# Twelve conditioning groups of a two-layer diffusion backbone: ten of them placed anew between attention, linear attention and three norms

## The reference

```python
def ada_mod(cond, w, b):
    mod = jax.nn.silu(cond) @ w + b
    return [m[:, None, :] for m in jnp.split(mod, 6, axis=-1)]
...
    for l in range(DEPTH):
        sc1, scl1, gc1, sc2, scl2, gc2 = ada_mod(cond_ctx, ada_w[l], ada_b[l])
        sl1, sll1, gl1, sl2, sll2, gl2 = ada_mod(c, ada_w[l], ada_b[l])
        hc = modulate(rmsnorm(xc, norm_mix[l]), sc1, scl1)
        hl = modulate(rmsnorm(xl, norm_mix[l]), sl1, sll1)
...
        xc = xc + gc1 * oc
        xl = xl + gl1 * ol
        xc = xc + gc2 * hier_moe(modulate(rmsnorm(xc, norm_ffn[l]), sc2, scl2), *moe)
        xl = xl + gl2 * hier_moe(modulate(rmsnorm(xl, norm_ffn[l]), sl2, sll2), *moe)
```

## Time and profile before

| | |
|---|---|
| times of the three runs | 1988.06, 2001.43, 2002.7 us; median 2001.43 |
| time of the profiled execution | 2004.93 us |
| its span in the trace | 2003.1 us, mean granted PE clock 0.892 |
| PE busy | 1653.6 us (83%), x14360 |
| DVE, ACT, POOL busy | 601.6 (30%), 466.1 (23%), 229.0 us (11%) |
| queue of the weight stream | 288.89 MB, 37.9% of the 16 engines' span |
| products of the 12 groups (L315) | 60.5 us, x768, idle before them 59.3 us |

### The profile page before, as it was taken

One profiled execution on the slowest core, in us unless ns is written; L12 is line 12 of the kernel. 1 busy time (PEld: TensorE's weight loads), 2 busy tenths in 40 slices (PEclk: granted clock), 3 DMA queues, 4 the chain that ended last, 5 costly groups with the idle time before them and its releaser, 6 DMA issues. The chain is left out here.

```text
span 2003.1 us, 35164 instructions
## 1 busy us (share of the span) xinstructions
PE 1653.6 (83%) x14360; PEld 1221.1 (61%) x14361; DVE 601.6 (30%) x1419; ACT 466.1 (23%) x1058; POOL 229.0 (11%) x218
## 2 busy tenths in 40 slices
PE   2996956849999999639995888888875799999991
PEld 1553544436788788415544777777753577877871
DVE  2005654140111111260023566766623201111114
ACT  2114511022000010020033556555412110100002
POOL 0000110000000000100007255555300000000001
PEclk8997987959999999759996789989987799999995
DMA  8323664400788888702300000000022048888862
GB/s 324 125 96 118 257 254 174 168 11 19 314 322 318 315 315 310 287 22 105 105 0 3 4 5 5 5 5 5 5 107 74 0 176 327 305 315 329 311 240 103
DMA packets 49921, 314.77 MB, mean 157 GB/s; under 512 B 6192, under 2 KB 9584, under 8 KB 14480
## 3 DMA queue, kind: packets, MB, share of 16 engines
q1 hardware_dynamic: 43200, 288.89, 37.9%
q10 hardware_dynamic: 4880, 17.96, 2.2%
q0 software_dynamic: 1728, 6.29, 0.9%
HBM read 298.05 MB, written 15.07 MB: 156 GB/s over the span
## 5 line engine op out<-in xcount | busy, mean ns | idle before, releaser
L1260 PEld LDWEIGHTS ps<-arena,ring 128*128 128x128 f32 x4096 | 468.3, 194 | 21.7 <-issue 21.7
L1260 PE MATMUL ps<-arena,ring 128*128 x4096 | 468.0, 277 | 5.3 <-issue 5.3
L1272 PE MATMUL ps<-ring,arena 128*96 128x512 f32 x512 | 225.0, 592 | 0.0
L292 PE MATMUL ps<-HT,ring 128*128 128x384 f32 x544 | 179.7, 494 | 15.5 <-PEq L358 8.2
L1332 DVE TENSOR_TENSOR arena<-arena,ps 128x96 f32<-128x96 f32 x128 | 32.6, 254 | 496.8 <-ACT arena L1299 496.8
L292 PEld LDWEIGHTS ps<-HT,ring 128*128 128x128 f32 x544 | 104.8, 193 | 90.0 <-issue 20.2
L1272 PEld LDWEIGHTS ps<-ring,arena 128*96 128x96 f32 x512 | 81.0, 163 | 119.2 <-issue 119.2
L292 PE MATMUL ps<-arena,ring 128*128 128x384 f32 x384 | 125.9, 492 | 23.7 <-DVEq L1525 23.7
L1299 ACT ACTIVATE arena<-ps 128x96 f32<-128x96 f32 x128 | 32.2, 251 | 476.7 <-PE ps L1260 476.5
L1359 POOL DMA_INDIRECT arena<-moe_rows,arena x12 | 11.6, 969 | 1059.0 <-DMA moe_rows<-arena 1056.0
L292 PEld LDWEIGHTS ps<-arena,ring 128*128 128x128 f32 x384 | 73.8, 193 | 76.3 <-DVEq L1525 24.8
(11 more groups left out here) (308 smaller groups left out, 1980.0 us busy)
## 6 DMA issues: line engine op xcount, KB each, us to landing
ring<-wstream SPq DMA_DIRECT2D x272, 1024.0 KB, 6.7
moe_rows<-arena ACTq DMA_DIRECT2D x32, 384.0 KB, 6.8
consts<-cst ACTq DMA_DIRECT2D x1, 1648.5 KB, 17.1
XT<-xT ACTq DMA_DIRECT2D x1, 1536.0 KB, 11.1
yT<-HT ACTq DMA_DIRECT2D x1, 1536.0 KB, 5.1
arena<-wa SPq DMA_DIRECT2D x1, 1024.0 KB, 4.8
arena<-rcst SPq DMA_DIRECT2D x2, 448.0 KB, 3.8
ring<-zrwkv SPq DMA_DIRECT2D x16, 32.0 KB, 2.0
```

What stands on the lines that cost most here:

```text
L292: mm = pe.matmul(bank(m % 8), w[:, k, m % 2 * P:m % 2 * P + P], rhs[:, k, :], start=k == 0, stop=k == KC - 1)
L1260: mm = pe.matmul(bank(f % 2, CAP, CAP * w), wt[:, k, f % 2 * P:f % 2 * P + P], TOK[:, k, bass.ds(first, CAP)], start=k == 0, stop=k == KC - 1)
L1272: mm = pe.matmul(bank(4 + j, 512)[0:CAP], HIDG[:, f, :], wt[:, f, :], start=f == 0, stop=f == 3)
```

## The change

Group by group: attention takes five groups (2 to 6) and in every fifth step from step 1 on, where it had four in every sixth from step 2 on; linear attention takes two (7 and 8) where it had three; the tail none where it had three; the norm before MoE 0 takes group 9; the first norm of layer 1 takes groups 10 and 11. The tiles are laid out in the new order: groups 2 to 8, the output projection, group 9, MoE 0, groups 10 and 11, RWKV. In a norm, the products of the first group stand before PE's sum, its `ada_act` after the squares, its turn behind the sum and its `ada_dve` between L463 and the wait for the root. The second group of a norm has its products and turn behind that on PE, its `ada_act` after the modulation of chunk 3 on ACT and its `ada_dve` at the end of DVE's order.

```diff
--- before.py
+++ after.py
@@ -53,15 +53,18 @@
 QUAD = 4
 N_QUADS = N_ADA // QUAD
 QUADS_NOW = 2
+QUADS_MIXER, QUADS_RKV = 7, 2
 N_IN = 10
 N_OUT = 4
 N_MOE = NE * 6
 AT_ADA = 0
 AT_IN = AT_ADA + QUAD * QUADS_NOW
 AT_ADA_LATE = AT_IN + N_IN
-AT_OUT = AT_ADA_LATE + N_ADA - QUAD * QUADS_NOW
-AT_MOE0 = AT_OUT + N_OUT
-AT_RKV = AT_MOE0 + N_MOE
+AT_OUT = AT_ADA_LATE + QUAD * QUADS_MIXER
+AT_ADA_LAST = AT_OUT + N_OUT
+AT_MOE0 = AT_ADA_LAST + N_ADA - QUAD * (QUADS_NOW + QUADS_MIXER + QUADS_RKV)
+AT_ADA_RKV = AT_MOE0 + N_MOE
+AT_RKV = AT_ADA_RKV + QUAD * QUADS_RKV
 AT_LORA = AT_RKV + 12
 AT_GATE = AT_LORA + 1
 AT_WO = AT_GATE + 1
@@ -414,7 +417,7 @@
                 ada_dve(dve, 1, 4)
                 dve.sem_inc(s_rs, 1)
 
-        def norm_block(l, w, end, save=None):
+        def norm_block(l, w, end, quads=()):
 
             n = norms[0]
             norms[0] += 1
@@ -428,6 +431,8 @@
                 def _(act):
                     for k in range(KC):
                         act.activation(HT[:, k, :], XT[:, k, :], ACT.Square).then_inc(s_sq, 1)
+                    for q in quads[:1]:
+                        ada_act(act, q, 2 + q % 2)
                     act.wait_ge(s_var, n + 1)
                     act.activation(VAR, VAR, ACT.Sqrt).then_inc(s_sd, 1)
                     for k in range(KC):
@@ -440,6 +445,11 @@
                             act_o.inc(act.activation(HT[:, k, a:b], HT[:, k, a:b], ACT.Identity,
                                                      bias=mod[:, l, 3 * w, k, c:c + 1],
                                                      scale=gain[:, l, w, k, c:c + 1]))
+                        if k == 3:
+                            for q in quads[1:2]:
+                                ada_act(act, q, 2 + q % 2)
+                    for q in quads[2:]:
+                        ada_act(act, q, 2 + q % 2)
                     act_o.wait()
                     if l is None:
                         act.dma_start(yT, HT_[:, :]).then_inc(out_sem, 16)
@@ -448,9 +458,15 @@
 
                 @block.tensor
                 def _(pe):
-
+                    for q in quads[:1]:
+                        ada_pe_products(pe, q, 2 + q % 2)
                     pe.wait_ge(s_sqs, n + 1)
                     pe.matmul(bank(0), ones, RS, start=True, stop=True).then_inc(s_ss, 1)
+                    for q in quads[:1]:
+                        ada_pe_turn(pe, q, 4 + q % 2)
+                    for q in quads[1:]:
+                        ada_pe_products(pe, q, 2 + q % 2)
+                        ada_pe_turn(pe, q, 4 + q % 2)
 
                 @block.vector
                 def _(dve):
@@ -461,10 +477,14 @@
                     dve.sem_inc(s_sqs, 1)
                     dve.wait_ge(s_ss, n + 1)
                     dve.tensor_scalar(VAR, bank(0), 1.0 / D, EPS, ALU.mult, ALU.add).then_inc(s_var, 1)
+                    for q in quads[:1]:
+                        ada_dve(dve, q, 4 + q % 2)
                     dve.wait_ge(s_sd, n + 1)
                     dve_o(dve.reciprocal(RS, VAR))
                     for k in range(KC):
                         dve.tensor_tensor(HT[:, k, :], XT[:, k, :], RS, ALU.mult).then_inc(s_xn, 1)
+                    for q in quads[1:]:
+                        ada_dve(dve, q, 4 + q % 2)
 
 
 
@@ -645,10 +665,10 @@
             def keys(b):
                 return CTX if b < 0 else T
 
-            first_quad, quads_here = QUADS_NOW, 4
+            first_quad, quads_here = QUADS_NOW, 5
 
             def quad_at(step, u):
-                q, at = divmod(u - 2 - step, 6)
+                q, at = divmod(u - 1 - step, 5)
                 return first_quad + q if at == 0 and 0 <= q < quads_here else None
 
             @block.sync
@@ -814,7 +834,7 @@
             def flat(v):
                 return v.rearrange("p r d t -> p (r d t)")
 
-            gla_quads = (6, 7, 8)
+            gla_quads = (7, 8)
 
             @block.sync
             def _(sp):
@@ -979,7 +999,6 @@
                                             sem("gla_variance_ready"), sem("gla_std_ready"))
         O4 = area(at_aq, 4 * T)
         SQ4 = area(at_aq + 4 * T, 4 * T)
-        tail_quads = (9, 10, 11)
         with nc.Block() as block:
             @block.sync
             def _(sp):
@@ -994,25 +1013,19 @@
                 dve.tensor_scalar(SQ4.rearrange("p (h t) -> p h t", h=4),
                                   ps[:, 0:2048].rearrange("p (h t) -> p h t", h=4)[:, :, 0:T],
                                   1.0 / GV, EPS, ALU.mult, ALU.add).then_inc(s_gv, 1)
-                ada_dve(dve, tail_quads[0], 4 + tail_quads[0] % 2)
                 dve.wait_ge(s_gsd, 1)
                 dve_o(dve.reciprocal(SQ4, SQ4))
                 dve_o(dve.scalar_tensor_tensor(out=SQ4, in0=SQ4, scalar=V[:, V_GNORM:V_GNORM + 1], in1=O4,
                                                op0=ALU.mult, op1=ALU.mult))
                 dve_o(dve.tensor_tensor(OT[:, 0:4].rearrange("p h t -> p (h t)"), SQ4, SG.rearrange("p h t -> p (h t)"),
                                         ALU.mult))
-                for q in tail_quads[1:]:
-                    ada_dve(dve, q, 4 + q % 2)
 
             @block.scalar
             def _(act):
                 act.wait_ge(s_go2, 1)
                 act.activation(SQ4, O4, ACT.Square).then_inc(s_gsq, 1)
-                ada_act(act, tail_quads[0], 6 + tail_quads[0] % 2)
                 act.wait_ge(s_gv, 1)
                 act.activation(SQ4, SQ4, ACT.Sqrt).then_inc(s_gsd, 1)
-                for q in tail_quads[1:]:
-                    ada_act(act, q, 6 + q % 2)
 
             @block.gpsimd
             def _(pool):
@@ -1020,15 +1033,10 @@
 
             @block.tensor
             def _(pe):
-                ada_pe_products(pe, tail_quads[0], 6 + tail_quads[0] % 2)
                 pe.wait_ge(s_gsq, 1)
                 for h in range(4):
                     mm = pe.matmul(bank(h), ones, SQ4[:, T * h:T * h + T], start=True, stop=True)
                 mm.then_inc(s_gss, 1)
-                ada_pe_turn(pe, tail_quads[0], 4 + tail_quads[0] % 2)
-                for q in tail_quads[1:]:
-                    ada_pe_products(pe, q, 6 + q % 2)
-                    ada_pe_turn(pe, q, 4 + q % 2)
 
 
         def out_block(l, at, src, end, name):
@@ -1470,11 +1478,11 @@
 
             return router_sems + expert_sems
 
-        norm_block(0, 1, AT_MOE0 + RING)
-        moe0_sems = moe_block(0, AT_MOE0, AT_RKV + RING)
-
-
-        norm_block(1, 0, AT_RKV + RING)
+        norm_block(0, 1, AT_MOE0 + RING, quads=(9,))
+        moe0_sems = moe_block(0, AT_MOE0, AT_ADA_RKV + RING)
+
+
+        norm_block(1, 0, AT_RKV + RING, quads=(10, 11))
         a_[0] = 0
         XX = area(take(KC * T), KC * T, k=KC, t=T)
         XM = [area(take(KC * T), KC * T, k=KC, t=T) for _ in range(2)]
@@ -2181,7 +2189,13 @@
 
 def ada_tile(q, j):
 
-    return AT_ADA + QUAD * q + j if q < QUADS_NOW else AT_ADA_LATE + QUAD * (q - QUADS_NOW) + j
+    if q < QUADS_NOW:
+        return AT_ADA + QUAD * q + j
+    if q < QUADS_NOW + QUADS_MIXER:
+        return AT_ADA_LATE + QUAD * (q - QUADS_NOW) + j
+    if q < N_QUADS - QUADS_RKV:
+        return AT_ADA_LAST + QUAD * (q - QUADS_NOW - QUADS_MIXER) + j
+    return AT_ADA_RKV + QUAD * (q - N_QUADS + QUADS_RKV) + j
 
 
 def cols(v):
@@ -2237,7 +2251,7 @@
     w_in = np.zeros((D, 2560), np.float32)
     w_in[:, :IN_W] = f["ev_w_in"][0]
     w[AT_IN:AT_ADA_LATE] = tiles_of(w_in)
-    w[AT_OUT:AT_MOE0] = tiles_of(f["ev_w_out"][0])
+    w[AT_OUT:AT_ADA_LAST] = tiles_of(f["ev_w_out"][0])
     for l, at in ((0, AT_MOE0), (1, AT_MOE1)):
         for e in range(NE):
             t = at + 6 * e

```

## The result

| | before | after |
|---|---|---|
| median of 20 runs | 1993.63 us | 2004.62 us |
| lowest and highest | 1984.88, 2003.15 | 1998.22, 2008.5 |
| ratio, 95% interval | | 1.0047 [1.0029, 1.0064], that is +9.4 us (+5.8 to +12.8) |
| span of the profiled execution | 2003.1 us | 2005.2 us |
| PE busy, granted clock | 1653.6 us, 0.892 | 1664.9 us, 0.889 |

What follows compares the result with a forecast made beforehand. Each block is bounded by the engine that ends last, with the weight stream held up by its ring. Terms 1.1 + 1.5 - 8.7 + 2.0 - 0.6 + 3.7 gave -1.0 us, from 2001.43 to 2000.4; range 1987 to 2009.

Steps and rivals of the forecast that it cites:

- PE's clock at that point: Linear attention's matrices: after over 5 us idle, PE runs some 3 us at 1.2 GHz; +1.5 us (0 to 1.5).
- Attention, +6.3 (4 to 7.6): Attention: one group more costs PE 4.1 us, plus a 2.2 us wait for tiles ahead of the second group.
- Linear attention's wait: Linear attention: DVE waits for group 7, whose tiles come late, making its chain 2.1 to 3.6 us longer.
- the row that the prediction named for it: Tail: clock 0.50 at the first products after 3.76 us idle, cited as showing the skill's rule on DMA waits.
- Tail, -8.7: Tail without groups: its end moves 8.4 us earlier to its own chain's end, and sum L1026 ends 0.3 earlier.
- Output projection, +2.0 (1.5 to 2.2): Output projection: PE starts at a low clock after an 18 us gap, costing 2.0 us.
- Norm before MoE 0, -0.6: Norm before MoE 0: group 9 is hidden and warms the sum, -0.7 us; the router's constants come 0.1 later.
- First norm of layer 1, +3.7 (1.7 to 5.5): Layer 1's first norm: group 10 gains 0.7 us; group 11's late tiles hold up ACT's modulation, 4.4 us with the copy.
- The one of the slower side: Attention, linear attention, norm: waits for tiles block PE, DVE and ACT queues; up to +6.3 us, 2008; chance 21%.
- the chain's upper 3.6: Linear attention: upper end of the lengthening of DVE's and ACT's chain, 2.1 to 3.6 us, taken as 2.8.
- the fast rival: Linear attention's matrices come at 274.1 (-3.4) and the clock stays up; down to -12.5 us, 1989; chance 27%.
- The rival that DVE's chain does not decide: Linear attention: its first group is ready when DVE arrives, and attention has no wait; -4 to -12 us, chance 27%.

Runs made afterwards that it cites:

- e10: Kernel after, with unread products on PE in all gaps of linear attention; 0.997 of the kernel before, -6.0 us.
- e4: Kernel after, with nine unread products on PE ahead of linear attention's matrices; 1.001 of the kernel before, +2.0 us.
- e7: e6 plus nine unread products on PE ahead of linear attention's matrices; 0.9945 of the kernel before, -11.0 us.
- e11: Kernel after, unchanged, executed again for a second profile; attention 79.3 us, matrices to tail 47.4 us.
- e1: Kernel before with only the mixer's part: five groups in attention, two in linear attention, three in tail, none in norms; 1.004, +8.0 us.
- e13: e9 with five groups in attention instead of four and one in the tail instead of two; 0.9906 of the kernel before.
- e3: Kernel before with only group 11 moved, from the tail to the norm before MoE 0; 0.9959, -8.2 us.
- e2: Kernel before with only the tail's groups moved: one to the norm before MoE 0, two to layer 1's first norm; 0.9984, -3.2 us.
- e5: Kernel before with the tail's three groups spread: one each in tail, norm before MoE 0 and layer 1's first norm; 0.9966, -6.8 us.
- e6: e5 with two groups in linear attention instead of three and two in the tail instead of one; 0.9961 of the kernel before, -7.8 us.
- e9: e7 plus unread products between matrices and state steps and ahead of each further state step; 0.9899 of the kernel before, -20.2 us.
- e14: e9 run once more, unchanged; 0.9875 of the kernel before, -24.9 us.
- e8: Kernel after with attention's five groups one step later (2, 7, 12, 17, 22); 1.0058 of the kernel before, +11.6 us.

## Why the prediction was wrong

The forecast named the moves and was wrong on their sizes. The misses of the stages, in the order of the table, are +1.8, +0.7, +4.4, -0.8, +0.8, -0.1, -1.1 and +1.8; they turn -1.0 into +6.4 at the last boundary, and the runs say +9.4. The largest, +4.4, is shown below to be PE's clock; the +1.8 of attention and of the first norm of layer 1 go with stretches at half clock, but no experiment took those away.

**The step that failed** is "PE's clock at that point". I priced the half clock at the start of the matrices, +1.5 (0 to 1.5), and let it be full behind them. The matrices cost just that: from their start to the first state step it is 293.40 - 283.38 = 10.0 us, against 286.24 - 277.51 = 8.7 in the trace of before. But the next step, to 306.56, takes 13.2 us where it took 8.7, with 7.09 us for 32 records of L993 that need 3.79 at full clock. The upper bound of that term was wrong: PE had come back to full clock during the matrices (L969 at 287.53 takes 1.56 us for 48 records), a gap of 2.91 us followed in which it waited for DVE, and the records behind it ran at 0.50. The kernel before has the same gap of 2.91 us and runs at 1.00 behind it. So the two parts cost +1.3 and +4.4 where the term had 1.5 in all. With the measured 5.9 in its place the sum would have been +3.4, the right direction. e10 shows the cause: filling the gaps, and nothing else, brings both parts back to what they were before, the whole stretch from 47.3 to 36.5 us, and the total from +9.4 to -6.0. That the removed group had kept the clock up fits the counts, though it isn't shown alone, since e4 and e7 put other work in its place and came out differently: all five profiles with three groups in linear attention read 41.4 or 41.5 us, the seven with two and no filler behind the matrices 42.7, 47.3, 47.4, and 50.2 or 50.3 in the other four.

**Attention, +6.3 (4 to 7.6):** +8.1 measured. The wait ahead of the second group was 0.95 us, less than the 2.2 of the sum. What I had not priced is the stretch at half clock from about 204 to 214 us: 10.3 us at 0.54 do the work of 5.6 at full clock, up to 4.7 lost. It stands in four of the six executions with this placement (after, e4, e10, e11, all 79.3 us); e1, with full clock there, took 74.9, and e13, with full clock there but a longer wait (2.55 us) and slower products ahead of it (6.29 us for the second group, 5.05 after), 78.4.

**Linear attention's wait:** right in kind. DVE waited 3.44 us for group 7 (forecast 2.1 to 3.6 for the chain), PE waits for DVE and not for a DMA ahead of the matrices, and the stretch from scans to matrices shrank by 4.5 us instead of the 12.9 of a group. The products took 5.35 us, the cold value. The Trainium skill (page "TensorE: Matmul & The Clock Gate", section "Loop structure matters more than you think") warns that long waits for DMA between matmuls leave PE at half rate. Here the waits were for DVE, 5.45 and 2.91 us, and the direction agrees (0.50 for 11.7 us of work at 293.3). But behind the same 2.91 us the kernel before had 1.00, so the rule alone doesn't tell which wait costs. I had let it weigh on the first microseconds only. Nor was the row that the prediction named for it a wait for DMA: the 3.76 us ahead of the tail's first products end at a block boundary (`PEq L813`).

**Tail, -8.7:** -9.5. L1038 took 4.55 us (forecast 4.4) and DVE's L1013 followed no later than before. The rest is a barrier that was 1.0 us shorter. e3 shows how the tail should be read: nearly all of the cost is its last group's.

**Output projection, +2.0 (1.5 to 2.2):** +2.8, above the upper bound. After a wait of 17.27 us the granted clock was 0.50 for the first 5.2 us and 0.82 in the next 1 us. Worked out from these windows that loses 2.8 us; the prediction had started from the 1.6 us that the input projection lost after 8.15 us.

**Norm before MoE 0, -0.6:** -0.7. The sum took 0.91 us, warm.

**First norm of layer 1, +3.7 (1.7 to 5.5):** +5.5. The mechanism is as written, ACT waited 4.66 us ahead of its fifth chunk (forecast 3.9); the missing part is that group 10's products took 6.30 us instead of 5.1 and so held up the sum behind them (L464 at 867.37), which stood 1.4 us past the end of DVE's sums (865.94) and delayed the whole norm. In the second execution they took 5.55 us and the stage 35.4. e2 (35.3 us) and e5 (30.5 us) show that the second group costs nearly all of it. One group alone, in e5, e6, e7, e9, e13 and e14, leaves 30.2 to 31.8 us, that is -0.3 to +1.3.

**The rivals.** The one of the slower side named the right queues and gave +6.3 as its end, with 21%. The measured +9.4 lies beyond that end. It got its size from waits; its clock terms were the short cold starts of the sum, and a clock that stays down should have been a rival of its own. That end is also added up too high: attention's upper 7.6 and the chain's upper 3.6 put the matrices at +3.2 and not +4.2, so it is +5.3. (Two more slips of the working: the fast rival's 274.1 comes out as 273.6, and the clock terms that it names, 1.5, 1.5 and 2.0, make 5.0 and not 4.6.) None of them changes the direction. The rival that DVE's chain does not decide did not come: the gap ahead of group 7 was there.

**What stays open.** What decides when the clock falls inside linear attention is not settled: e4 and e7 had the same products ahead of the matrices and differ by 7.5 us behind them. That work in all the gaps keeps it up is shown in four executions (e9, e10, e13, e14: 36.5 to 37.8 us). The kernel before with these products in its gaps wasn't run, so how much of e9's gain is the placement and how much it would have had from them alone is known only by stages: of the 20 us between its boundaries and those of before, 3.6 lie between matrices and tail. Why attention's clock fell at 204 us in four executions of this placement and not in e1 and e13 (nor in e8, one step later) isn't known, and nothing was tried to hold it up there. The 3 us between boundaries and runs were not located.

## What to carry to other kernels

A piece of work that only waits for its own weights may be what keeps TensorE's clock up for the critical work behind it; before moving it, price everything up to the next long busy stretch at half clock, not the first microseconds. Of several equal jobs behind a chain those that end after the chain cost most, so move those first: here one of three gave 8.9 of 9.5 us. A job that is put in front of others in an in-order queue needs its inputs in the ring before the block begins; the first group in a norm did and cost -0.3 to +1.3 us, the second did not and cost about 5. The best version run here, four groups in attention, two each in linear attention and tail, one in each norm, and PE kept busy through linear attention's gaps, is 1.0 to 1.25% faster than the kernel before, which has no such work in its gaps.

## What the runs showed of the hardware that was not expected

- The same 32 records of 128x64 took 3.79 us at a granted clock of 1.00 and 7.09 at 0.50, with PE busy almost throughout (293.3 to 305.1 after). In the earlier trace rows the clock rose while the products ran; here it stayed at half through 11.7 us of work, and in e7 through 23.42 us of work in a window of 25.2.
- PE waited 1.32 us (e7), 1.06 (e9) and 1.09 (e14) in the middle of 48 like records for nothing that the profile shows. In e4, e10 and e13, the same instructions at another place of the program, it did not.
- The time behind RWKV's first matmul scatters by 19 us over executions of kernels that are the same there.
